# Four reorderings in a hybrid encoder layer: the state recurrence before the within-chunk sums, residual rows loaded tile by tile, a fifth transpose before the first products, and one root for the last four tiles of the first FFN

## The chip, the cores and the metric

The kernel runs on one core of one Trainium2 chip. The metric is the device time of one execution in microseconds (us); less is better. The engines are named as the profile names them: PE is TensorE (matmul), PEld its weight load, DVE is VectorE, ACT is ScalarE, POOL is GpSimd, SP is SyncE, which issues the DMA transfers.

## The reference

One layer works on 1024 rows of 1024 float32 values.

```python
h = h + 0.5 * swiglu(rmsnorm(h, g1), w_gate1, w_up1, w_down1)      # first FFN, width 2816
n = rmsnorm(h, g_mix); z = n @ w_in
# z -> c_q (256) | c_kv (128) | k_rope (32) | u (512) | gate_attn (1024) | gate_ssm (1024)
attn = mla_attention(c_q, c_kv, k_rope)                            # 8 heads, not causal
# S5: 32 groups of 16 inputs, 64 complex states each, in both directions of the sequence
x_t = B u_t;  s_t = lam * s_{t-1} + x_t;  y_t = Re(C s_t);  y = y_fwd + y_bwd + D * u
ssm = glu(gelu(y) @ w_glu + b_glu)
h = h + (sigmoid(gate_attn) * (attn @ w_oa) + sigmoid(gate_ssm) * (ssm @ w_os)) @ w_out
h = h + 0.5 * swiglu(rmsnorm(h, g2), w_gate2, w_up2, w_down2)      # second FFN
out = rmsnorm(h, g_final)
```

## The kernel before

The sequence is cut into 8 tiles of 128 rows (ST = 8), the width into 8 blocks of 128 (KT = 8). A float32 product is made of three passes over operands split into a high part, rounded for the PE, and a low part, the rest (`three_passes`, lines 48 to 50): hi times hi, hi times lo, lo times hi. ACT makes high parts (copies), DVE or POOL low parts (subtractions). All orders are written out by hand, one program per engine, and semaphores link them. DMA transfers all go out on SP's one queue. The phases run one after the other with a barrier between them:

- **First FFN** (`ffn_phase`, 0 to 727 us). A Strassen-like scheme of seven products with operands in blocks. At its start the rows are normalised: squares on ACT (L904), variance on DVE (L371), a root on ACT (L375), one Newton step of five small instructions on DVE (L98 to L102), and the scaling of a tile (`scaled`, L1069). Tiles 0 to 3 are turned (transposed by PE, L1343) as they are, tiles 4 to 7 enter sums of blocks that POOL makes (`combine`, L1310 to L1315). PE's order is: two blocks of tiles 0 to 3 turned, product (0,0), product (0,2), sums of tile 4 turned, product (1,0), sums of tile 5, product (1,2), sums of tiles 6 and 7, then the first whole matrix (`matrix(0)`). The second FFN is the same function with `loaded` set: tiles 0 to 3 come normalised from the phase before it, and tiles 4 to 7 take one root together.
- **Projection** (`project_phase`, 727 to 832 us). `Norm` turns eight tiles in the order 4, 5, 6, 7, 0, 1, 2, 3, counted as turns 0 to 7. Turns 0 to 3 need no scaling first. `RowProduct` multiplies by rows of the weight, a unit (one block of 128) at a time. For its first four units PE does the tiles of the first four turns, with turns 4 to 7 put in between, then the rest of the tiles.
- **SSM** (`ssm_phase`, 832 to 1087 us). Chunks of 8 rows (T = 8), 128 chunks. PE transposes u, makes the chunk states (L1697, ACT writes them into H by L1735 and L1736), and the sums within a chunk, 8 quarters of them (`within`, L1709; DVE adds them to u, L1793). DVE runs the recurrence over chunks: 127 steps of three dependent instructions (L1800, L1802, L1804). ACT (`forward`, L1752) and DVE (`backward`, L1811) then lay the states out for PE's output product y (L1724). Beside this, 16 gate products (`side`, a `ColumnProduct` of 48 matmuls each) go through PE; each needs a sigmoid on ACT (L1628), a high part two products ahead (`high`, ACT L165), a low part on POOL (L173) and stores of the gates. C_mat, which shares its space with M, the matrix of the within sums, is loaded by one transfer of 4 MB (L1678) when the within sums are done; SP issues the gates' stores after it.
- **Mixer** (attention, 1087 to 1458 us), not touched.
- **Merge** (`merge_phase`, 1458 to 1605 us). For each of 8 blocks PE multiplies the attention by w_o_attn (`woa`, 24 matmuls), DVE multiplies by a gate (L2539) and adds the SSM part (L2542); a slot of psum is free for product n + 2 when the gate is multiplied in. Then w_out, 16 units of 24 matmuls. The residual rows (`rows`) come back from DRAM (`kept`) by one transfer of 4 MB (L2468) in SP's second round, and are first read at unit 8 (`add`, L2454).
- **Second FFN** (1605 to 2279 us).

Of the kernel before, what the change touches and what calls it, by code (L numbers as in the profile page):

```python
# [32 lines left out]
P = 128  # L33
# [3 lines left out]
ST = SEQ // P  # L37
# [230 lines left out]
class Norm:  # L268
# [22 lines left out]
    def act(self, act, rp):  # L291
        rest = slice(0, ST - self.AHEAD)
        self.act_square(act, ST - self.AHEAD - 1)
        self.act_high(act, 0)
        act.wait_ge(self.s_var, 1)
        act.activation(self.stat[:, 2, rest], self.stat[:, 1, rest], ACT.Sqrt).then_inc(self.s_sqrt, 1)
        for i in range(1, self.AHEAD):
            self.act_high(act, i)
        for n in range(2):
            rp.high(act, n)  # L300
        for i in range(self.AHEAD, ST):
            self.act_high(act, i)
            if i < ST - 2:
                rp.high(act, i - 2)
# [23 lines left out]
    def dve(self, dve, rp):  # L328
        st, rest = self.stat, slice(0, ST - self.AHEAD)
        dve.wait_ge(self.s_sq, 1)  # L330
        dve.tensor_scalar(st[:, 1, rest], st[:, 0, rest], 1.0 / D, EPS, ALU.mult, ALU.add).then_inc(self.s_var, 1)
        self.dve_low(dve, 0)
        dve.wait_ge(self.s_sqrt, 1)
        newton(Chain(dve, self.s_rstd), st[:, 1, rest], st[:, 2, rest], st[:, 3, rest], st[:, 4, rest])
        dve.wait_ge(self.s_gain, 16)
        self.dve_rows(dve, 4)
        for i in range(1, self.AHEAD):
            self.dve_low(dve, i)
        rp.low(dve, 0)
        self.dve_rows(dve, 5)  # L340
        rp.low(dve, 1)
        for i in range(self.AHEAD, ST):
            self.dve_low(dve, i)
            if i < ST - 2:
                self.dve_rows(dve, i + 2)
                rp.low(dve, i - 2)
# [362 lines left out]
def ffn_phase(nc, tag, gain, w_gate, w_up, w_down, rows, ident, psum, hidden, residual, x=None, finish=None, tables=None, ahead=0, following=None, loaded=None):  # L709
# [10 lines left out]
    with Phase(nc) as ctx:  # L720
# [177 lines left out]
        def _(act):  # L898
# [11 lines left out]

            def lows_high(i):
                for m in range(QUAD):
                    act.wait_ge(s_tr, low_turned(m, i))
                    act.copy(B_hi[:, LOW_BLOCKS[i], :, tile(m)], blocks(LOW_BANKS[i][m])).then_inc(s_bhi, 1)
# [67 lines left out]
            if not ahead:  # L982
                squares(0)
                squares(1)
# [3 lines left out]
            if loaded:  # L988
                square(ST - 1)
                norm.root(act, 0, slice(QUAD, ST))  # L990
            else:
                high(0, 0)
                squares(2)
# [3 lines left out]
            if not loaded:  # L997
                squares(3)
# [57 lines left out]
        def _(dve):  # L1056
# [60 lines left out]
            if loaded:  # L1117
                dve.wait_ge(s_sq, SQUARES)
                norm.var(dve, 0, slice(QUAD, ST))
                norm.inverse(dve, 0, slice(QUAD, ST))  # L1120
                scaled(QUAD)
                scaled(QUAD + 1)
            else:
                low(0, 0)
                normalised(2)
            lows_low(1)
            low(0, 2)
            if loaded:
                scaled(QUAD + 2)
                scaled(QUAD + 3)  # L1130
            else:
                normalised(3)
# [326 lines left out]
def project_phase(nc, w, rows, ident, psum, nT_hi, nT_lo, u, kept, latent_rows, trig_rows, E_dram, carry):  # L1459


    with Phase(nc) as ctx:
# [114 lines left out]
        def _(pe):  # L1577
            ahead, rest = norm.TILES[:norm.AHEAD], norm.TILES[norm.AHEAD:]
            for i in range(norm.AHEAD):
                norm.pe(pe, i)  # L1580
            for n in range(rp.S):
                if n == 0:
                    pe.wait_ge(norm.s_lo, norm.AHEAD)
                rp.tiles(pe, n, ahead, rest[-1])
                for i in ((4,), (5,), (6, 7), ())[n]:
                    norm.pe(pe, i)
# [50 lines left out]
GATES_AFTER = (13, 14, None, 15)  # L1637


def ssm_phase(nc, w, rows, rows_at, ident, psum, nT_hi, nT_lo, u, gates, kern_dram, C_dram, lam8_dram):  # L1640
# [5 lines left out]
    with Phase(nc) as ctx:  # L1646
# [19 lines left out]
        def _(sp):  # L1666
            side.gp.load(sp, 0)
            sp.dma_start(Db, w["ssm_d"][0:1, :].rearrange("a (g i) -> a g i", i=SG).broadcast_to([P, GROUPS, SG])).then_inc(s["d"], 16)
# [4 lines left out]
            sp.dma_start(lam8[:].rearrange("p a b g -> p (a b g)"), lam8_dram).then_inc(s["lam"], 16)  # L1673
# [8 lines left out]
        def _(pe):  # L1682
# [20 lines left out]
            for q in range(NQ):  # L1703
                if q < 4:
                    pe.wait_ge(s["ec"], 2 * (2 * NQ - 3 + q))
                else:
                    pe.wait_ge(s["wadd"], q - 3)
                for g in range(4 * q, 4 * q + 4):
                    mm = pe.matmul(psum[:, 4 + q % 4, g % 4 * P:(g % 4 + 1) * P], UT[:, g, :], M[:, g, :], start=True, stop=True)  # L1709
                mm.then_inc(s["within"], 1)  # L1710
            pe.wait_ge(s["wadd"], NQ)
            for n in range(1, GATES_FIRST):
                side.gp.product(pe, n)
# [16 lines left out]
        def _(act):  # L1730
# [27 lines left out]
            for n in range(GATES_FIRST - 1):  # L1758
                side.sigmoid(act, n)
                if n == GATES_FIRST - 5:  # L1760
# [23 lines left out]
        def _(dve):  # L1784
# [4 lines left out]
            for q in range(NQ):  # L1789
# [6 lines left out]
            for n in range(CH - 1):  # L1796
# [7 lines left out]
                dve.tensor_tensor(H[:, n + 1], H[:, n + 1], prod[:, 1, ::-1], ALU.add).then_inc(s["scan"], 1)  # L1804
            dve.wait_ge(s["scan"], CH)
# [603 lines left out]
def merge_phase(nc, w, psum, rows, kept, woa, held, loaded, gates, partial, gain):  # L2409

    with Phase(nc) as ctx:
# [16 lines left out]
        s_sum, s_hi, s_lo, s_kept = sem("sum"), sem("hi"), sem("lo"), sem("kept")  # L2428
# [26 lines left out]

        def bank(i, half):
# [3 lines left out]
        def _(sp):  # L2460
            for n in range(KT):
# [5 lines left out]
                if n == 1:  # L2467
                    sp.dma_start(rows[:], kept.rearrange("(m p) d -> p m d", p=P)).then_inc(s_kept, 16)  # L2468
# [3 lines left out]
            for u in range(2, NU):  # L2472
                load(sp, u)
                if u == 2:
# [54 lines left out]
        def _(dve):  # L2529
# [19 lines left out]
            for u in range(2, NU):  # L2549
                low(dve, u)  # L2550
                if u == KT:
                    dve.wait_ge(s_kept, 16)
# [10 lines left out]
                if u in (KT + 4, KT + 5):  # L2563
                    i = u - KT - 4
                    dve.wait_ge(s_sq, 2 * i + 2)
                    norm.var(dve, i, slice(2 * i, 2 * i + 2))
            for i in range(QUAD):
# [102 lines left out]
```

## Time and profile before

| | |
|---|---|
| median of 3 runs | 2278.45 us (2277.05 to 2278.88) |
| the profiled execution | 2281.39 us, its span 2279.3 us |
| PE busy | 2150.0 us, 94% of the span, 10074 matmuls |
| DVE busy | 1468.7 us, 64% |
| ACT busy | 918.1 us, 40% |
| POOL busy | 611.4 us, 27% |
| DMA | 263.00 MB, mean 115 GB/s |

The profile gives each instruction's start, duration, engine and line, and for an idle stretch the engine or transfer that ended it. PE is the busiest engine in every phase; what an edit is worth is read from the stretches in which PE stands idle.

### The profile page before, as it was taken

The page shows a single profiled execution, that of the slowest core. Times are in us where ns is not written, and L with a number is a line of the kernel's source. Part 1 is how long each engine was busy: PE and PEld are TensorE (multiplying, and loading weights), DVE is VectorE, ACT ScalarE, POOL GpSimd, SP SyncE. Part 2 cuts the span into 40 slices and gives each one's busy share as a digit, 9 for nine tenths or more (in the row PEclk, how much of TensorE's full clock was granted, in tenths as well). Part 3 has the DMA queues.
Part 4 walks back from the last instruction along what each step waited for, and adds up shares of the span by engine and source line. Part 5 has one row for each costly group of instructions (what it writes and reads, how often), then busy time and mean ns, then how long its engine had stood idle before and what let it go on. Part 6 is the DMA issues. An engine that isn't in the chain of part 4 may idle for free. (4 is left out here: it accounts for less than half of the span.)

```text
span 2279.3 us, 27668 instructions
## 1 busy us (share of the span) xinstructions
PE 2150.0 (94%) x10074; PEld 1778.2 (78%) x10074; DVE 1468.7 (64%) x2300; ACT 918.1 (40%) x1551; POOL 611.4 (27%) x510
## 2 busy tenths in 40 slices
PE   5899999999998999959899999889899999999997
PEld 4778888887887998848777887778678888887886
DVE  7787667657777426951457887554766565657777
ACT  5423333324445342124426778422532323224444
POOL 5336877740000021201002333100533333310000
PEclk9999999999998999979999999999999999999999
DMA  3423334349333455311430000273123232349333
GB/s 120 107 89 122 118 117 139 122 171 339 97 112 114 135 86 163 97 42 55 131 130 25 7 6 15 93 257 126 56 88 120 88 121 88 120 148 342 101 97 111
DMA packets 234471, 263.00 MB, mean 115 GB/s; under 512 B 34720, under 2 KB 169376, under 8 KB 233824
## 3 DMA queue, kind: packets, MB, share of 16 engines
q1 hardware_dynamic: 234336, 261.23, 36.1%
q8 instruction: 81, 1.33, 0.2%
q14 instruction: 54, 0.44, 0.1%
HBM read 184.60 MB, written 76.58 MB: 115 GB/s over the span
## 5 line engine op out<-in xcount | busy, mean ns | idle before, releaser
L48 PE MATMUL psum<-f_B_hi,f_A_hi 128*128 128x512 f32 x1232 | 488.4, 396 | 24.7 <-DVE f_A_lo L1053 12.9
L50 PE MATMUL psum<-f_B_hi,f_A_lo 128*128 128x512 f32 x1232 | 483.3, 392 | 0.0
L49 PE MATMUL psum<-f_B_lo,f_A_hi 128*128 128x512 f32 x1232 | 483.0, 392 | 0.0
L48 PEld LDWEIGHTS psum<-f_B_hi,f_A_hi 128*128 128x128 f32 x1232 | 233.5, 190 | 76.5 <-DVE f_A_lo L1053 20.1
L50 PEld LDWEIGHTS psum<-f_B_hi,f_A_lo 128*128 128x128 f32 x1232 | 233.3, 189 | 49.4
L49 PEld LDWEIGHTS psum<-f_B_lo,f_A_hi 128*128 128x128 f32 x1232 | 233.6, 190 | 47.6
L939 ACT CAST f_A_hi<-f_S 128x512 fp32r<-128x512 f32 x176 | 109.3, 622 | 348.4 <-PE psum L50 340.3
L48 PE MATMUL psum<-f_wd,f_hh 128*128 128x512 f32 x616 | 240.4, 390 | 3.6 <-DVE f_wd L1099 3.6
L50 PE MATMUL psum<-f_wd,f_hh 128*128 128x512 f32 x616 | 240.4, 390 | 0.0
L49 PE MATMUL psum<-f_wd,f_hh 128*128 128x512 f32 x616 | 240.3, 390 | 0.0
L1328 POOL TENSOR_TENSOR f_S<-f_raw 128x512 f32<-128x512 f32 x86 | 129.9, 1511 | 304.4 <-DVE f_A_lo L1053 284.2
L973 ACT CAST f_hh<-f_h_raw 128x512 fp32r<-128x512 f32 x154 | 96.0, 623 | 240.4 <-PE psum L50 230.3
L1053 DVE TENSOR_TENSOR f_A_lo<-f_raw,f_A_hi 128x512 fp32r<-128x512 f32 x132 | 134.8, 1022 | 69.4 <-ACT f_A_hi L939 68.6
L1097 DVE TENSOR_TENSOR f_hh<-f_h_raw,f_hh 128x512 fp32r<-128x512 f32 x154 | 106.6, 692 | 105.0 <-ACT f_hh L973 104.1
L1053 DVE TENSOR_TENSOR f_A_lo<-f_S,f_A_hi 128x512 fp32r<-128x512 f32 x176 | 142.9, 813 | 3.6 <-ACT f_A_hi L939 2.6
L48 PEld LDWEIGHTS psum<-f_wd,f_hh 128*128 128x128 f32 x616 | 116.1, 188 | 28.6 <-DVE f_wd L1099 4.4
L939 ACT CAST f_A_hi<-f_raw 128x512 fp32r<-128x512 f32 x132 | 81.9, 620 | 137.0 <-PE psum L50 135.2
L50 PEld LDWEIGHTS psum<-f_wd,f_hh 128*128 128x128 f32 x616 | 116.0, 188 | 24.2
L49 PEld LDWEIGHTS psum<-f_wd,f_hh 128*128 128x128 f32 x616 | 116.0, 188 | 24.1
L48 PE MATMUL psum<-nT_hi,ga_hi 128*128 128x512 f32 x256 | 103.1, 403 | 24.2 <-POOL ga_lo L173 23.4
L2262 DVE TENSOR_TENSOR mx_PT_lo<-psum,mx_PT_hi 128x512 fp32r<-128x512 f32 x128 | 87.8, 686 | 47.4 <-ACT mx_PT_hi L2126 46.9
L1099 DVE TENSOR_TENSOR f_wd<-f_wd_raw,f_wd 128x512 fp32r<-128x512 f32 x154 | 105.7, 686 | 0.0
(335 smaller groups left out, 4191.7 us busy)
## 6 DMA issues: line engine op xcount, KB each, us to landing
f_h_raw<-hidden SPq DMA_DIRECT2D x154, 256.0 KB, 2.6
hidden<-rows SPq DMA_DIRECT2D x44, 768.0 KB, 4.7
f_raw<-ffn_w_gate SPq DMA_DIRECT2D x44, 512.0 KB, 5.2
f_raw<-ffn_w_up SPq DMA_DIRECT2D x44, 512.0 KB, 5.0
f_wd_raw<-ffn_w_down SPq DMA_DIRECT2D x44, 512.0 KB, 8.9
rows<-x SPq DMA_DIRECT2D x16, 512.0 KB, 7.4
ga_raw<-w_in SPq DMA_DIRECT2D x16, 512.0 KB, 4.6
gates<-ga_sig SPq DMA_DIRECT2D x32, 256.0 KB, 2.3
```

The costliest lines, as they stand in the source:

```text
L48: pe.matmul(out, lhs_hi, rhs_hi, start=first, stop=False, skip_group_check=go_on)
L49: pe.matmul(out, lhs_hi, rhs_lo, start=False, stop=False, skip_group_check=go_on)
L50: return pe.matmul(out, lhs_lo, rhs_hi, start=False, stop=last, skip_group_check=go_on)
L939: act.copy(A_hi[:, q], src).then_inc(s_hi, 1)
L973: act.copy(hh[v % 2][0][:], h_raw[v % 8][:]).then_inc(s_dhi, 1)
L1053: eng.tensor_tensor(A_lo[:, q], src, A_hi[:, q].bitcast(F32), ALU.subtract).then_inc(s_lo, 1)
L1097: dve.tensor_tensor(hh[v % 2][1][:], h_raw[v % 8][:], hh[v % 2][0][:].bitcast(F32), ALU.subtract).then_inc(s_dlo, 1)
L1099: dve.tensor_tensor(wd[v % 2][1][:], wd_of(q, k), wd[v % 2][0][:].bitcast(F32), ALU.subtract).then_inc(s_dlo, 1)
L1328: pool.tensor_tensor(S[:, i], a, b, op).then_inc(s_sum, 1)
L2262: dve.tensor_tensor(pt(PT_lo, g, x), turned_bank(x), pt(PT_hi, g, x).bitcast(F32), ALU.subtract).then_inc(s["tr_lo"], 1)
```

## The change

**First FFN.** An ACT Sqrt of one column stands ahead of the first squares, so that the root's table is loaded there. The variance, root and Newton step of tiles 4 and 5 and those of tiles 6 and 7 become one of each for the four tiles, after all four squares.

**Projection.** Turn 4 is done before the first unit, and one turn follows each of the first three units (before: one, one, two). ACT and DVE follow that order.

**SSM.** The recurrence starts when the states are there; the eight within additions on DVE stand inside it, after steps 10 to 13 and 28 to 31. On PE gate product 1 stands between the fourth and the fifth quarter of the within sums, and products 2 to 12 no longer wait for the additions. lam is loaded second instead of after ten other transfers. On ACT the first two `forward` stand after sigmoid 11 (before: after sigmoid 8).

**Merge.** The residual rows come as eight transfers of 0.5 MB: tiles 0 to 3 in rounds 4 to 7, tiles 4 to 7 with units 7 to 10.

```diff
 class Norm:                                  # projection
-        for n in range(2):
-            rp.high(act, n)
         for i in range(self.AHEAD, ST):
+            rp.high(act, i - self.AHEAD)
             self.act_high(act, i)
-            if i < ST - 2:
-                rp.high(act, i - 2)
...
-        rp.low(dve, 0)
-        self.dve_rows(dve, 5)
-        rp.low(dve, 1)
         for i in range(self.AHEAD, ST):
+            rp.low(dve, i - self.AHEAD)
+            if i + 1 < ST:
+                self.dve_rows(dve, i + 1)
             self.dve_low(dve, i)
-            if i < ST - 2:
-                self.dve_rows(dve, i + 2)
-                rp.low(dve, i - 2)
...
-            for i in range(norm.AHEAD):
+            for i in range(norm.AHEAD + 1):
                 norm.pe(pe, i)
...
-                for i in ((4,), (5,), (6, 7), ())[n]:
-                    norm.pe(pe, i)
+                if norm.AHEAD + 1 + n < ST:
+                    norm.pe(pe, norm.AHEAD + 1 + n)
 ffn_phase, ACT (first FFN: loaded is None)
+            def other_squares():
+                for m in range(ST - 1 if loaded else QUAD, ST):
+                    square(m)
+                norm.root(act, 0 if loaded else 2, slice(QUAD, ST))
...
             if not ahead:
+                act.activation(stat[:, 2, 0:1], ident[:, 0:1], ACT.Sqrt)
                 squares(0)
                 squares(1)
             lows_high(0)
-                squares(2)
+            other_squares()
             lows_high(1)
...
-            if not loaded:
-                squares(3)
 ffn_phase, DVE
-                normalised(2)
+            dve.wait_ge(s_sq, SQUARES)
+            norm.var(dve, 0 if loaded else 2, slice(QUAD, ST))
+            norm.inverse(dve, 0 if loaded else 2, slice(QUAD, ST))
+            scaled(QUAD)
+            scaled(QUAD + 1)
             lows_low(1)
             low(0, 2)
-                normalised(3)
+            scaled(QUAD + 2)
+            scaled(QUAD + 3)
 ssm_phase
+WITHIN_AFTER = (10, 11, 12, 13, 28, 29, 30, 31)
...
             for q in range(NQ):
+                if q == NQ // 2:
+                    side.gp.product(pe, 1)
...
-            pe.wait_ge(s["wadd"], NQ)
-            for n in range(1, GATES_FIRST):
-                side.gp.product(pe, n)
+            for n in range(2, GATES_FIRST):
+                side.gp.product(pe, n)
+            pe.wait_ge(s["wadd"], NQ)
...
                 side.sigmoid(act, n)
-                if n == GATES_FIRST - 5:
+                if n == GATES_FIRST - 2:
                     forward(0)
                     forward(1)
...
+                if n in WITHIN_AFTER:
+                    within(WITHIN_AFTER.index(n))
 merge_phase, SP
+        def take(sp, m):
+            sp.dma_start(rows[:, m, :], kept[m * P:(m + 1) * P, :]).then_inc(s_kept[m // QUAD], 16)
...
-                if n == 1:
-                    sp.dma_start(rows[:], kept.rearrange("(m p) d -> p m d", p=P)).then_inc(s_kept, 16)
+                if n >= QUAD:
+                    take(sp, n - QUAD)
...
+                if KT - 1 <= u < KT + 3:
+                    take(sp, u - KT + 1 + QUAD)
```

ACT in the SSM phase, before: sigmoids of the gates (`ga_sig`), high parts of the gate weights (`ga_hi`) and the four copies of `forward` (`rows<-ss_H`). The first sigmoid row shown is that of product 8.

```order
L1628 ACTIVATE ga_sig<-psum 128x512 x2
L165 CAST ga_hi<-ga_raw 128x1024
L1752 COPY rows<-ss_H 64x128x8 x4
L1628 ACTIVATE ga_sig<-psum 128x512 x2
L165 CAST ga_hi<-ga_raw 128x1024
```

The same engine after the change, from the sigmoid of product 10 on.

```order
L1618 ACTIVATE ga_sig<-psum 128x512 x2
L165 CAST ga_hi<-ga_raw 128x1024
L1618 ACTIVATE ga_sig<-psum 128x512 x2
L165 CAST ga_hi<-ga_raw 128x1024
L1745 COPY rows<-ss_H 64x128x8 x4
L1618 ACTIVATE ga_sig<-psum 128x512 x2
L165 CAST ga_hi<-ga_raw 128x1024
```

The four copies have moved down past three pairs of sigmoid and high part, so that the high parts for products 11, 12 and 13 no longer stand behind them.

SP in the merge phase, before, from its second round on: gates, the SSM part (`mg_part`), w_o_attn (`woa_raw`), the residual rows and w_out (`mg_wo_raw`).

```order
L2464 DMA mg_gate<-gates 128x1024
L2465 DMA mg_part<-partial 128x1024
L157 DMA woa_raw_11138<-w_o_attn 128x4x128
L2468 DMA rows<-kept 128x8x1024
L2464 DMA mg_gate<-gates 128x1024
L2465 DMA mg_part<-partial 128x1024
L157 DMA woa_raw_11139<-w_o_attn 128x4x128
```

SP in the same phase after the change, from the fifth round on; in the second there is no such row any more.

```order
L2462 DMA mg_gate<-gates 128x1024
L2463 DMA mg_part<-partial 128x1024
L157 DMA woa_raw_11124<-w_o_attn 128x4x128
L2452 DMA rows<-kept 128x1024
L2462 DMA mg_gate<-gates 128x1024
L2463 DMA mg_part<-partial 128x1024
L2452 DMA rows<-kept 128x1024
```

The rows' 4 MB no longer stand between the gates of block 1 and those of block 2; one tile goes out in each of the last four rounds.

DVE at the start of the first FFN after the change, from the low part of product (0,0) on (before, a second set of variance and Newton rows, L371 and L98 to L102, stood ahead of the last row here, and these rows were 128x2).

```order
L1048 TENSOR_TENSOR f_A_lo<-f_raw_74,f_A_hi 128x512
L365 TENSOR_SCALAR f_stat<-f_stat 128x4
L98 RECIPROCAL f_stat<-f_stat 128x4
L99 TENSOR_TENSOR f_stat<-f_stat 128x4
L100 TENSOR_TENSOR f_stat<-f_stat 128x4
L101 TENSOR_SCALAR f_stat<-f_stat 128x4
L102 TENSOR_TENSOR f_stat<-f_stat 128x4
L1064 SCALAR_TENSOR_TENSOR rows<-rows,f_stat,f_gb 128x1024 x2
L1077 TENSOR_TENSOR f_B_lo<-psum,f_B_hi 128x4x128 x4
L1048 TENSOR_TENSOR f_A_lo<-f_raw_74,f_A_hi 128x512
L1064 SCALAR_TENSOR_TENSOR rows<-rows,f_stat,f_gb 128x1024 x2
```

The second Newton step is gone, and its tiles are scaled straight after the low part of product (0,2).

## Rows read from the trace of the kernel before

**Rows 1.** Longest wait of PE in the SSM phase: total, times, longest (us).

```profile
PE psum L48 <- POOL ga_lo L173: 23.4, 1, 23.4
```

**Rows 2.** Timeline of the SSM phase: start, duration (us), engine, operation, [idle before, releaser].

```profile
865.77 7.30 PE L1709 MATMUL psum<-ss_C_mat,ss_UT 128*128 128x128 f32 x64
...
873.93 0.50 PE L48 MATMUL psum<-nT_hi,ga_hi 128*128 128x512 f32 x1 [0.85 <-DVE u L1793]
...
1010.05 0.79 PE L48 MATMUL psum<-nT_hi,ga_hi 128*128 128x512 f32 x1 [23.40 <-POOL ga_lo L173]
...
1035.12 3.73 PE L1724 MATMUL psum<-ss_C_mat,rows 128*128 128x128 f32 x32
...
857.75 0.58 ACT L1736 COPY ss_H<-psum 64x512 f32<-64x512 f32 x1
...
888.99 1.17 ACT L1628 ACTIVATE ga_sig<-psum 128x512 f32<-128x512 f32 x2 [21.00 <-DMA gates<-ga_sig]
...
998.40 7.34 ACT L1752 COPY rows<-ss_H 64x1024 f32<-64x1024 f32 x4 [32.17 <-DVE ss_H L1804]
...
873.11 0.37 SPq L1678 DMA_DIRECT2D ss_C_mat<-C_dram  x1
873.52 16.98 SPq L1612 DMA_DIRECT2D gates<-ga_sig  x4
...
891.17 2.40 POOL L173 TENSOR_TENSOR ga_lo<-ga_raw,ga_hi 128x1024 fp32r<-128x1024 f32 x1 [20.73 <-ACT ga_hi L165]
...
873.19 0.69 DVE L1793 TENSOR_TENSOR u<-psum,u 128x512 f32<-128x512 f32 x1 [0.20 <-PE psum L1709]
873.80 0.28 DVE L1800 TENSOR_TENSOR ss_prod<-ss_H,ss_lam 128x128 f32<-128x128 f32 x1
```

**Rows 3.** Busy times in the recurrence's stretch: PE, PEld, DVE, ACT, POOL, clock, DMA, GB/s.

```profile
873.80:998.40 124.60, 112.72 (x480) 90.32 (x480) 111.54 (x383) 16.27 (x25) 19.37 (x8) 0.97 0.34 106
```

**Rows 4.** The recurrence's first instruction: ns min/median/max, first and last start (us).

```profile
L1800 DVE TENSOR_TENSOR ss_prod<-ss_H,ss_lam x127: 281/293/2479, 873.8 to 997.5; 128x128 f32<-128x128 f32 x127
```

**Rows 5.** Timeline of the merge phase, then the w_out matmuls (ns min/median/max, starts).

```profile
1469.33 1.08 SPq L2468 DMA_DIRECT2D rows<-kept  x1
...
1489.47 1.22 DVE L2539 TENSOR_TENSOR mg_val<-psum,mg_gate 128x1024 f32<-128x1024 f32 x1 [9.37 <-DMA mg_gate<-gates]
...
1490.84 0.77 PE L48 MATMUL psum<-aT_hi,woa_hi 128*128 128x512 f32 x1 [7.73 <-DVE mg_val L2539]
...
L48 PE MATMUL psum<-mg_wo_hi,mg_mT_hi x128: 389/389/389, 1515.5 to 1601.9; 128*128 128x512 f32 x128
```

**Rows 6.** Busy times in ten us of the merge, columns as in rows 3.

```profile
1475.00:1485.00 10.00, 8.11 (x36) 6.38 (x34) 4.88 (x5) 2.58 (x4) 0.00 (x0) 1.00 1.03 406
```

**Rows 7.** Timeline of the projection, PE.

```profile
742.73 1.03 PE L360 MATMUL psum<-ident,pjn_xn 128*128 128x128 f32 x8
743.52 0.45 PE L48 MATMUL psum<-rp_hi,nT_hi 128*128 128x448 f32 x1
...
747.86 0.47 PE L48 MATMUL psum<-rp_hi,nT_hi 128*128 128x448 f32 x1 [0.79 <-DVE rp_lo L242]
...
754.97 0.47 PE L48 MATMUL psum<-rp_hi,nT_hi 128*128 128x448 f32 x1
```

**Rows 8.** Timeline of the first FFN's start, ACT, DVE and PE.

```profile
21.19 1.06 ACT L904 ACTIVATE f_dump<-rows 128x1024 f32<-128x1024 f32 x1
22.15 0.19 ACT L904 ACTIVATION_READ_ACCUMULATOR f_dump<-rows 128x1 f32 x1
...
23.80 2.48 DVE L1069 SCALAR_TENSOR_TENSOR rows<-rows,f_stat,f_gb 128x1024 f32<-128x1024 f32 x2
...
57.95 0.47 PE L48 MATMUL psum<-f_B_hi,f_A_hi 128*128 128x512 f32 x1 [1.76 <-DVE f_B_lo L1087]
```

**Rows 9.** Timeline of the second FFN's start, DVE and PE.

```profile
1612.11 2.48 DVE L1069 SCALAR_TENSOR_TENSOR rows<-rows,f_stat,f_gb 128x1024 f32<-128x1024 f32 x2
...
1640.32 0.47 PE L48 MATMUL psum<-f_B_hi,f_A_hi 128*128 128x512 f32 x1 [1.19 <-DVE f_B_lo L1087]
```

More of the change, by code:

```diff
@@ L987, in _ @@
             lows_high(0)
[L988 to L991, printed above, removed]
+            if not loaded:
                 high(0, 0)
-                squares(2)
+            other_squares()
             lows_high(1)
@@ L1116, in _ @@
             lows_low(0)
[L1117 to L1123, printed above, removed]
-                low(0, 0)
-                normalised(2)
+            if not loaded:
+                low(0, 0)
+            dve.wait_ge(s_sq, SQUARES)
[3 more added lines that the diff above has]
+            scaled(QUAD + 1)
             lows_low(1)
             low(0, 2)
[L1128 to L1131, printed above, removed]
-                normalised(3)
+            scaled(QUAD + 2)
+            scaled(QUAD + 3)
             low(1, 0)
@@ L1667, in _ @@
             side.gp.load(sp, 0)
+            sp.dma_start(lam8[:].rearrange("p a b g -> p (a b g)"), lam8_dram).then_inc(s["lam"], 16)
             sp.dma_start(Db, w["ssm_d"][0:1, :].rearrange("a (g i) -> a g i", i=SG).broadcast_to([P, GROUPS, SG])).then_inc(s["d"], 16)
@@ L1672, in _ @@
             side.gp.load(sp, 1)
-            sp.dma_start(lam8[:].rearrange("p a b g -> p (a b g)"), lam8_dram).then_inc(s["lam"], 16)
             side.gp.load(sp, 2)
@@ L1788, in _, with within @@
             dve.memset(H[:, 0], 0.0).then_inc(s["scan"], 1)
-            for q in range(NQ):
+            def within(q):
                 g = slice(4 * q, 4 * q + 4)
@@ L2427, in merge_phase @@
         s_g, s_p = [sem("g0"), sem("g1")], [sem("p0"), sem("p1")]
-        s_sum, s_hi, s_lo, s_kept = sem("sum"), sem("hi"), sem("lo"), sem("kept")
+        s_sum, s_hi, s_lo, s_kept = sem("sum"), sem("hi"), sem("lo"), [sem("kept0"), sem("kept1")]
         NU = 2 * KT
@@ L2551, in _ @@
                 if u == KT:
-                    dve.wait_ge(s_kept, 16)
+                    dve.wait_ge(s_kept[0], 16 * QUAD)
                     for i in range(QUAD):
@@ L2566, in _ @@
                     norm.var(dve, i, slice(2 * i, 2 * i + 2))
+            dve.wait_ge(s_kept[1], 16 * QUAD)
             for i in range(QUAD):
```

## Prediction

> **What bounds the kernel now.** I read the busy times first: PE is busy for 94% of the span, so time can only come from where PE stands idle. The lists of waits, phase by phase, name two large holes: 23.4 us in the SSM phase, ended by a low part of the gate weights [rows 1], and 7.73 us in the merge, ended by a gate multiplication on DVE [rows 5]. I then followed both back on the timelines, and after them the small holes at the starts of the projection and of the first FFN. The reader should see that neither of the large holes is made by the engine named as its releaser.
>
> In the SSM phase, gate product 11 starts at 1010.05. Its weights need ACT's high part, which ACT makes after sigmoid 9; but ACT had waited 32.17 us in front of `forward` for the end of the recurrence at 998.4, and then copied for 7.34 us [rows 2]. So PE's hole is the recurrence's end, and the recurrence began only at 873.80, after the within additions, although the states were there at 858.33 (857.75 + 0.58) [rows 2].
>
> In the merge, the multiplication waited until 1489.47 for its gates; these had been issued behind the 4 MB of residual rows of 1469.33 [rows 5].
>
> **The change part by part: the SSM phase.** PE's work stays the same; I lay it out again from the first within sum at 865.77 [rows 2]. One gate product is 112.72/10 = 11.27 us [rows 3], all within sums are 7.30 [rows 2].
>
> 1. Removed: the hole of 23.40, and the 0.85 before product 1, where PE waited for the last addition [rows 2]. PE can put product 1 between the quarters, as its low part was ready in time before too, and the fifth quarter needs psum banks that DVE frees after recurrence steps 10 to 13.
> 2. The recurrence is on nobody's path any more. It now starts at 858.4. Its step is 0.85 us where POOL is idle (three instructions of which the first is 0.29 [rows 4], with the gaps between them); 127 steps are 107.3. It took 124.6 [rows 3]: the 17.3 above that belong to the 8 POOL instructions in that stretch [rows 3], 2.16 each, and one first instruction took 2479 ns instead of 293 [rows 4]. Starting earlier it meets 11 of them: 858.4 + 107.3 + 11 x 2.16 + 8 additions of 0.69 [rows 2] = 995. The additions at steps 10 to 13 come at about 870 to 875, the others at about 890, both after PE has made their sums and before PE needs the banks again.
> 3. Added, a wait that the edit doesn't mention. The load of C_mat must wait for the last within sum, which now stands behind product 1: 11.27 later, at 884.4 instead of 873.11 [rows 2]. The gates' stores are queued behind that load on SP. Before, sigmoid 1 waited for the store of gates 0 until 888.99, after 21.00 us of idling, though the store was issued at 873.5 [rows 2]; its low part for product 3 was done at 891.17 + 2.40 = 893.57 [rows 2]. All of that moves by 11.27, to 904.84. Product 2 ends at 865.77 + 7.30 + 2 x 11.27 = 895.6. So PE stands idle for 9.2 us ahead of product 3. Before, product 2 ended at 873.93 + 22.54 = 896.47, 2.9 us after the low part was done.
> 4. The clock. After the hole of 23.40, products 11 and 12 took 1035.12 - 1010.05 = 25.07 [rows 2] where two full-speed ones take 22.54: 2.5 us at the lower of TensorE's two levels. The new hole should cost the same, so this cancels. If 9.2 us of idling cost nothing, there are 2.5 more to gain.
> 5. `forward` now follows sigmoid 11. Product 11 ends at 1008.7, the sigmoid and high part take 2.1, so the first pair of copies is done at about 1014.5 and all four at 1018.2. PE wants the first pair when product 12 ends.
>
> The y products then start at 865.77 + 7.30 + 12 x 11.27 + 9.2 + 2.5 = 1020.0 instead of 1035.12: **15.1 us**. If the store did not have to wait for the load, it would be 24.3, or 26.8 with the clock; that is the upper bound. What follows y is tied to it by the same waits as before and moves along.
>
> The Trainium skill (DMA: Bandwidth & Descriptors, "Queues, rings and completion order") says that descriptors of one issuing engine's row are consumed in ring order on each DMA engine, while a later transfer's completion need not come after an earlier one's. By the first half the wait of 9.2 us stands in full; by the second the gates' small store could get out earlier and the 24.3 would hold. The trace agrees with the first half here: the store took until 888.99. I give the second case little.
>
> **The merge.** Without the 4 MB, gates 2 stand behind the 2.5 MB of the first two rounds, issued from 1466.5 on. At 406 GB/s [rows 6] these and the 1.25 MB of the third round take 9.2 us from about 1467, so gates 2 land by 1478. DVE was through with block 1 at 1489.47 - 9.37 = 1480.1 [rows 5]; it can multiply by 1481.3, before product 3 ends at 1483.1 (1490.84 - 7.73) [rows 5]. The hole of 7.73 goes. After it, products 4 to 7 took 1515.5 - 1490.84 = 24.7 [rows 5]; 96 matmuls at the pace of w_out's, (1601.9 - 1515.5)/127/3 = 0.227, are 21.8. The 2.9 are the lower clock and go too. Together **10.6 us**. The eight small loads go out in rounds whose data are 1.5 MB or less per 5.4 us and are needed 50 us later; they are hidden. If gates 2 or 3 still came late, half of it would remain: I bound this part by 5 and 11.
>
> **The projection.** The fifth turn moves into the gap while PE waits for the first low part, at no cost: its scaled rows exist by then. From 742.73 to 754.97 PE now does four turns of 0.79 (743.52 - 742.73), three units of some 2.55, and holes of 0.79 and about 0.6 [rows 7]. After the change it does three turns, and since scaling and low parts run one turn ahead, each is ready when PE asks, by my walk through the waits: the tightest is the low part of the fourth unit, at 750.0 for 750.3. That is 0.8 + 0.8 + 0.5 = **2.1 us**, a little rounded down. Bounds: 0.8 (only the turn) and 3.5 (with less time at the lower clock before it).
>
> **The first FFN.** The table load that moves is hidden by the waiting for x, except some 0.3 us at the end of the first root's chain. The single root makes tile 4 later and tiles 6 and 7 sooner. ACT adds two squares, 1.25 us each (22.15 + 0.19 - 21.19) [rows 8], so the scaling of tile 4 starts at 23.80 + 2.5 - 0.3 = 26.0. How long from there to the first whole matrix? The second FFN already runs in this order: 1640.32 - 1612.11 = 28.2 [rows 9]. That gives 54.2 instead of 57.95 [rows 8]: **3.7 us**. Bounds: 1, if POOL's chain of block sums, which starts 2.2 later, binds more here, and 5. If the late tile 4 is all that counts, it is a loss of 2.2.
>
> **Sum.** 15.1 + 10.6 + 2.1 + 3.7 = 31.5 us. The profiled execution (2281.39, span 2279.3) would come to 2249.9; it stands 2.9 above the median. From the median, 2278.45 - 31.5 = **2247**.
>
> **The rivals.**
> - *The store gets past the load* (no wait for product 3). For it: nothing in the trace. 2278.45 - 31.5 - 9.2 = 2238, with the clock 2235. 0.07.
> - *The first FFN pays for its late tile 4*: 2247 + 3.7 + 2.2 = 2253. For it: PE is idle right before product (0,2), which needs no tile 6 or 7. Against it: [rows 9]. 0.12.
> - *The merge keeps a wait*, because w_out's and the part's transfers delay the gates: 2247 + 5 = 2252, at most 2256. 0.09.
> - *The other side: the recurrence still binds, and later than before.* It would have to end so late that y starts 31.5 after 1020.0, at 1051.5; with 3.7 for the first two copies that is an end at 1047.8, a recurrence of 189 us instead of 136.6. Its 381 instructions would have to be 0.14 us longer each, through POOL or through additions waiting inside it. From 1016.3 on (1020.0 - 3.7) each us is lost; above 1047.8 the kernel is slower than before, e.g. 2283 at 1052. Against it: the steps' times [rows 3, 4]. 0.02.
>
> **How the numbers follow.** My forecast, all parts within some us of the sum, has 0.68, with a range of its own of 2241 to 2252; the rest (0.02) is what I have not thought of. What a measurement can tell from no change is about 0.2%, 4.6 us. To leave out no more than 2 in 10, the range goes from 2238 (the store free) to 2256 (a merge wait or a loss in the FFN). Faster 0.96, within 0.2% 0.02, slower 0.02.
>
> **What would show it.** In the changed kernel: no wait above 1 us for product 11, a wait of about 9 us for product 3, ended by POOL's low part, and ahead of it ACT waiting for a gates transfer until about 900; the recurrence from 858 to 995; y at 15 us less distance from the first within sum; no wait in the merge's products; the projection's rest starting 10.1 after its first unit ends; the first whole matrix near 54. The prediction fails if the wait for product 3 is absent or much longer, or if the recurrence ends after 1016.

## The result, and the profile of the changed kernel

The changed kernel takes 2244.39 us (median of 4 runs, 2243.45 to 2245.89), the kernel before 2277.84 us beside it (4 runs, 2277.05 to 2278.88). The ratio is 0.9854, with a 95% interval of 0.9836 to 0.9871: 33.45 us less, 31.5 forecast. The profiled execution (2243.45 us, span 2241.4) is 37.9 us shorter in span than before's profiled one. The 4.45 us between 33.45 and 37.9 are taken up below.

TensorE's waits in the SSM phase come first, engine and line, then the releaser: us in total, times, longest. They answer to [rows 1]. The SSM phase begins at 825.36 us here and at 832.93 in before, so 7.6 us have to be added to a time of this phase to set it beside the forecast's.

```profile
PE psum L48 <- POOL ga_lo L173: 9.1, 1, 9.1
PE psum L1678 <- PEq L69: 1.5, 1, 1.5
```

The hole of 23.4 us is gone and one of 9.1 stands in its place, ended by the same line. The timeline of the same phase shows that it is another one (it answers to [rows 2]).

```profile
861.33 0.61 PE L1702 MATMUL psum<-ss_C_mat,ss_UT 128*128 128x128 f32 x4
861.70 0.48 PE L48 MATMUL psum<-nT_hi,ga_hi 128*128 128x512 f32 x1
...
897.07 0.80 PE L48 MATMUL psum<-nT_hi,ga_hi 128*128 128x512 f32 x1 [9.09 <-POOL ga_lo L173]
...
1011.01 0.50 PE L1717 MATMUL psum<-ss_C_mat,rows 128*128 128x128 f32 x3
...
876.77 0.37 SPq L1669 DMA_DIRECT2D ss_C_mat<-C_dram  x1
877.18 16.83 SPq L1602 DMA_DIRECT2D gates<-ga_sig  x4
...
892.49 1.17 ACT L1618 ACTIVATE ga_sig<-psum 128x512 f32<-128x512 f32 x2 [32.06 <-DMA gates<-ga_sig]
893.56 1.04 ACT L165 CAST ga_hi<-ga_raw 128x1024 fp32r<-128x1024 f32 x1
...
894.67 2.34 POOL L173 TENSOR_TENSOR ga_lo<-ga_raw,ga_hi 128x1024 fp32r<-128x1024 f32 x1 [31.80 <-ACT ga_hi L165]
...
1001.87 7.82 ACT L1745 COPY rows<-ss_H 64x1024 f32<-64x1024 f32 x4
```

Read it backwards from 897.07: product 3 waits for POOL's low part of 894.67, this for ACT's high part, ACT for the landing of the gates' first store, and that store was issued at 877.18, just behind the 4 MB load of C_mat at 876.77. The sigmoid that waits for it starts 15.3 us after its issue. The load was issued when the last within sum was done, and this now stands behind product 1 (861.70). The first copies (L1745) no longer wait for anything: the recurrence had ended by then.

The recurrence's first instruction (ns min/median/max, first and last start; as [rows 4]), and VectorE's copies that follow its end:

```profile
L1793 DVE TENSOR_TENSOR ss_prod<-ss_H,ss_lam x127: 280/293/2499, 850.9 to 984.9; 128x128 f32<-128x128 f32 x127
...
985.71 4.74 DVE L1806 COPY rows<-ss_H 64x1024 f32<-64x1024 f32 x4
```

It lasts 985.7 - 850.9 = 134.8 us. The forecast was 136.6.

Then busy times and granted clock (columns as in [rows 3]) of the first product behind the hole and of the last 25 us of products:

```profile
897.10:908.40 11.30, 11.30 (x43) 9.04 (x44) 10.18 (x33) 1.04 (x1) 2.40 (x1) 0.86 0.37 108
985.70:1011.00 25.30, 25.30 (x109) 20.34 (x108) 4.74 (x4) 11.72 (x10) 4.80 (x2) 1.00 0.29 84
```

The projection's start (as [rows 7]) and the first whole matrix of the first FFN (as the last of [rows 8]), TensorE's timeline:

```profile
54.08 0.47 PE L48 MATMUL psum<-f_B_hi,f_A_hi 128*128 128x512 f32 x1 [1.19 <-DVE f_B_lo L1082]
...
724.40 6.17 PE L354 MATMUL psum<-ident,rows 128*128 128x128 f32 x32 [4.71 <-PEq L69]
732.12 1.07 PE L354 MATMUL psum<-ident,pjn_xn 128*128 128x128 f32 x8 [1.55 <-DVE nT_lo L323]
734.91 0.44 PE L48 MATMUL psum<-rp_hi,nT_hi 128*128 128x448 f32 x1 [1.73 <-DVE rp_lo L242]
```

The fifth turn (732.12) stands ahead of the first unit (734.91), and the unit's wait is 1.73 us. In the merge TensorE's list of waits has one row left, the phase change; the 7.73 of [rows 5] is absent:

```profile
PE psum L48 <- PEq L69: 1.2, 1, 1.2
```

### The profile page after: what moved, and what is told of

Read it like the earlier page. It is cut to its first block and busy times, and to the rows that moved or that the text cites. A ratio compares the mean times of both kernels' runs of the same rounds, so it can differ in the third digit from the quotient of the medians.

```text
span 2241.4 us, 27668 instructions
## 1 busy us (share of the span) xinstructions
PE 2140.1 (95%) x10074; PEld 1770.1 (79%) x10074; DVE 1468.3 (66%) x2294; ACT 917.6 (41%) x1550; POOL 611.3 (27%) x510
```

## The experiments

Twelve kernels, each timed beside the kernel before. Each profile also gives the lengths of the stages, from one phase's first TensorE instruction to the next one's, so a stage that an experiment leaves alone is measured again by it. The expectations stand as they were written ahead of the runs.

**1. The SSM part alone** (p1): before, with the change's hunks of the SSM phase.

```diff
+                if q == NQ // 2:
+                    side.gp.product(pe, 1)
...
-                if n == GATES_FIRST - 5:
+                if n == GATES_FIRST - 2:
                     forward(0)
...
+                if n in WITHIN_AFTER:
+                    within(WITHIN_AFTER.index(n))
```

> Before, with the change's SSM part alone. Theory A (the parts are separate holes of TensorE and add up): the y products start 16.6 us sooner after the first within sum, as in the changed kernel, with a wait of about 9 us for gate product 3; the kernel gains 15.1 (forecast) to 16.6 us. Theory B (the parts lean on each other, as by the clock or by transfers): less than 13 or more than 19 us, and the rest of the 33.5 us is spread otherwise over the other three kernels of this set.

Measured: 2260.49 us against 2277.02, ratio 0.9928 (0.9914 to 0.9941), 16.5 us. Its profile has a wait of 8.49 us for product 3. Theory A. Behind that wait product 3 takes 13.97 us (903.35 to 917.32, granted clock 0.79), where in the changed kernel it takes 12.73 behind 9.09 us of idling (897.07 to 909.79, clock 0.88) and at full clock 11.25.

**2. The merge part alone** (p2).

```diff
-                if n == 1:
-                    sp.dma_start(rows[:], kept.rearrange("(m p) d -> p m d", p=P)).then_inc(s_kept, 16)
+                if n >= QUAD:
+                    take(sp, n - QUAD)
...
+                if KT - 1 <= u < KT + 3:
+                    take(sp, u - KT + 1 + QUAD)
```

> Before, with the residual rows tile by tile alone. Theory A: the wait of 7.73 us in the merge's products is gone and the clock stays up behind it; w_out's products start 10.6 to 10.8 us sooner after the merge's first product; gain 10.6 us. Theory B (only the wait goes, the granted clock is low there anyway): 7.7 us.

Measured: 2268.76, ratio 0.9964 (0.9951 to 0.9976), 8.3 us, which by itself lies between the two theories. The merge's products run from 1466.61 to w_out's first at 1504.77 without a wait, 38.2 us, as in the changed kernel. The other executions show what 10.6 was made of. The first product behind the hole, in p1, where the merge is as in before:

```profile
1471.75 0.76 PE L48 MATMUL psum<-aT_hi,woa_hi 128*128 128x512 f32 x1 [6.97 <-DVE mg_val L2544]
```

There the wait is 6.97 us and the four products behind it take 23.7 (to 1495.49), while in before's profile they are 7.73 and 24.7 [rows 5]. Over the eight profiles with the old merge, its first product to the second FFN's first turn is 139.17 us in before's and 137.25 to 137.61 in the seven others; over the five with the new one 128.3 to 128.4. The gain is 9.1 us from a usual execution and 10.8 only from the one that was profiled. The extra 1.7 us of before's profile lie in the clock behind the hole: 0.88 over its 24.7 us (p1: 0.91 over 23.75), and the four products there take 23.3 to 23.9 us in the seven others. So theory A is right in its mechanism (the wait and the clock both go), and its size is 9.1.

**3. The projection part alone** (p3).

```diff
-            for i in range(norm.AHEAD):
+            for i in range(norm.AHEAD + 1):
                 norm.pe(pe, i)
...
+            rp.low(dve, i - self.AHEAD)
+            if i + 1 < ST:
+                self.dve_rows(dve, i + 1)
             self.dve_low(dve, i)
```

> Before, with the projection's fifth turn sooner alone. Theory A (what the changed kernel's profile showed belongs to this edit: a shorter wait for the first low part and a first unit at the full granted clock): 4.2 us. Theory B (the full clock there was that one execution's, or comes from elsewhere): the forecast's 2.1 to 2.3 us. The profile's first unit tells it: 2.7 us long by A, 4.6 by B.

Measured: 2271.94, ratio 0.9981 (0.9972 to 0.9990), 5.1 us; the stage is 100.93 us long, where the eight profiles without the new order of turns have 104.7 to 105.5 (mean 105.2). The first unit takes 2.5 us (738.29 to the turn at 740.79), as theory A has it; 4.2 us by the stage.

**4. The first FFN's part alone** (p4).

```diff
+                act.activation(stat[:, 2, 0:1], ident[:, 0:1], ACT.Sqrt)
...
-                squares(2)
+            other_squares()
...
-                squares(3)
...
-                normalised(2)
...
+            norm.inverse(dve, 0 if loaded else 2, slice(QUAD, ST))
...
-                normalised(3)
```

> Before, with the first FFN's single root and early table load alone. Theory A (forecast): the first whole matrix starts at about 54.1 instead of 57.95, gain 3.4 to 3.9 us. Theory B (what the FFN gains at its start is partly given back by its end, as the changed kernel's projection started only 3.4 us sooner): 3 us or less.

Measured: 2275.33, ratio 0.9993 (0.9984 to 1.0002), 1.7 us and not told apart from nothing. The whole matrix starts at 54.31, as theory A has it, but the projection's first turn is at 725.59, 2.2 us sooner than in before. Over all profiles that turn is at 726.75 to 729.08 (mean 727.75, eight without the single root) and at 724.40 to 725.80 (mean 724.98, six with the single root): 2.8 us. A's start of the matrix is there, and the gain is B's (3 us or less); why some of it is not seen at the end of the phase, which B calls given back, is not shown.

**5. The copies' place alone** (s1): one line of before. It asks whether the recurrence had to start sooner at all.

```diff
-                if n == GATES_FIRST - 5:
+                if n == GATES_FIRST - 2:
                     forward(0)
                     forward(1)
```

> Before, with one edit alone: the copies of the states for the y products move on ScalarE from behind sigmoid 7 to behind sigmoid 10, two sigmoids later than they now ask for the end of the recurrence; the recurrence stays behind the within sums, as in before. Theory A (the 23.4 us hole was only ScalarE's queue; the recurrence at 998.4 is soon enough for everyone else): gate product 11 starts at about 986.7, product 12 ends at 1009.2, the y products follow without a wait, so 1035.1 - 1009.2 = 25.9 us gained and no new wait for product 3, since the load of C_mat keeps its place: 2251. Theory B (the recurrence has to start early, as the change makes it): the end at 998.4 is now waited for by the y products or their copies, and the gain is that of the SSM part alone, 16.5 us, or less: 2260 or more.

(In the kernel's own count, from 0, the copies move from behind sigmoid 8 to behind sigmoid 11.)

Measured: 2252.55 against 2278.15, ratio 0.9891 (0.9874 to 0.9908), 25.6 us. This one line gives more than the change's whole SSM part. In its timeline:

```profile
1008.67 0.42 PE L1724 MATMUL psum<-ss_C_mat,rows 128*128 128x128 f32 x2
...
1004.50 2.03 ACT L1752 COPY rows<-ss_H 64x1024 f32<-64x1024 f32 x1 [4.86 <-DVE ss_H L1804]
```

and of the recurrence's stretch (columns as in [rows 3]):

```profile
873.50:1004.46 130.96, 130.84 (x559) 105.20 (x560) 117.93 (x382) 22.31 (x33) 26.69 (x11) 1.00 0.40 125
```

TensorE works through, and the y products start at 1008.67. The copies still wait 4.86 us for the recurrence, but nobody waits for the copies. It is close: the recurrence ends at 1004.5 instead of 998.4, since with the hole gone it meets 11 POOL instructions instead of 8 [rows 3], (130.96 - 124.60)/3 = 2.1 us each; two copies of 1.96 (7.82 for four in the changed kernel) then end at 1008.4, 0.3 before y. Theory A, with almost no margin. The opposite single edit, the early recurrence with the copies left where they were, was not run, so what it would give alone is not shown.

**6. Sums first** (s2): the changed kernel, the within sums' additions at the recurrence's first steps.

```diff
-WITHIN_AFTER = (10, 11, 12, 13, 28, 29, 30, 31)
+WITHIN_AFTER = (0, 1, 2, 3, 8, 9, 10, 11)
...
-                if q == NQ // 2:
-                    side.gp.product(pe, 1)
...
-            for n in range(2, GATES_FIRST):
+            for n in range(1, GATES_FIRST):
```

> The changed kernel, with the additions of the within sums at steps 0 to 3 and 8 to 11 of the recurrence instead of 10 to 13 and 28 to 31, and gate product 1 behind all within sums again. The last within sum, and with it the load of C_mat, comes about 11 us sooner. Theory A (product 3 waits because the gates' store is queued behind the load of C_mat): the wait of 9.1 us for product 3 goes, and 1.3 us of lower clock with it: 2244.4 - 10.4 = 2234. Theory B (the store or its sigmoid is slow for another reason, e.g. the eleven POOL instructions that meet the recurrence): the wait stays where it is, 2243 to 2245, or only part of it goes.

Measured: 2234.71 against 2278.15, ratio 0.9811 (0.9796 to 0.9826), 9.7 us below the changed kernel's median (which was taken in another set, with before at 2277.84). SP's and ACT's rows:

```profile
869.48 0.37 SPq L1669 DMA_DIRECT2D ss_C_mat<-C_dram  x1
869.89 1.70 SPq L1602 DMA_DIRECT2D gates<-ga_sig  x2
...
885.71 1.17 ACT L1618 ACTIVATE ga_sig<-psum 128x512 f32<-128x512 f32 x2 [23.23 <-DMA gates<-ga_sig]
```

The sigmoid still starts 15.8 us after the store's issue, but both are early enough: the low part is done at 890.35 (887.89 + 2.46), product 2 ends at 891.77, and no product waits. The within sums pay 1.1 us in three small waits. Theory A.

**7. C_mat in four pieces behind the stores** (s3): the changed kernel, only SP's queue differs.

```diff
...
-            sp.dma_start(C_mat[:], C_dram.rearrange("c p g x -> p c g x")).then_inc(s["c"], 16)
-            side.sync(sp)
+            for b in range(BLOCKS):
+                if b >= 2:
+                    side.gp.load(sp, b + 2)
+                side.store(sp, b)
+                at = slice(PB * b, PB * b + PB)
+                sp.dma_start(C_mat[:, :, at], C_dram.rearrange("c p g x -> p c g x")[:, :, at]).then_inc(s["c"], 16)
+            side.sync(sp, BLOCKS)
...
-            pe.wait_ge(s["c"], 16)
+            pe.wait_ge(s["c"], 16 * BLOCKS)
```

> The changed kernel, with the 4 MB load of C_mat issued in four pieces of 1 MB, one behind each of the gates' stores 0 to 3, instead of whole ahead of them. Theory A (as in the run before, the store waits in the queue for the load): no wait above 1 us for product 3, the y products 10.4 us sooner: 2234. Theory B (4 MB beside the gates' stores delay them wherever they stand): the wait is only moved, to products 4 to 6, in pieces of 2 to 3 us: 2238 to 2244.

Measured: 2233.57, ratio 0.9806 (0.9791 to 0.9820), 10.8 us below the changed kernel's median and the fastest kernel of this study. Its queue, ACT and TensorE:

```profile
877.01 0.81 SPq L1602 DMA_DIRECT2D gates<-ga_sig  x2
877.87 0.46 SPq L1674 DMA_DIRECT2D ss_C_mat<-C_dram  x1
...
879.12 0.60 ACT L1618 ACTIVATE ga_sig<-psum 128x512 f32<-128x512 f32 x1 [18.45 <-DMA gates<-ga_sig]
...
1000.52 0.39 PE L1722 MATMUL psum<-ss_C_mat,rows 128*128 128x128 f32 x2
```

The same store, issued at nearly the same time (877.01 for 877.18), now lets the sigmoid start after 2.1 us instead of 15.3, and TensorE runs from the first within sum to y without a stop. Theory A; B's small waits are absent.

**8. The rest of the change with before's SSM phase and the one line of s1** (s4).

> The changed kernel's projection, first FFN and merge, with the SSM phase of before but for the copies for the y products, which stand behind sigmoid 10. Theory A (as above: the early recurrence buys nothing): 25.9 - 16.6 = 9.3 us below the changed kernel, 2235. Theory B (the early recurrence is needed): 2244 or above.

Measured: 2237.07, ratio 0.9822 (0.9807 to 0.9836), 7.3 us below the changed kernel; y starts at 1001.45, the copies wait 4.86 us for the recurrence. Theory A, 2 us above its figure. These 2 us do not lie in the SSM phase, which is as long as in s1 (228.68 us both times); in this profile the second FFN and its end take 674.2 us, the most of all fourteen.

**9 and 10. The first FFN's two edits apart** (t1: the early table load, t2: the single root).

```diff
+                act.activation(stat[:, 2, 0:1], ident[:, 0:1], ACT.Sqrt)
```

> Before, with the first FFN's table load ahead of its squares alone (one small square root on ScalarE before x is there). Theory A (forecast: hidden but for some 0.3 us): first whole matrix at about 57.6 instead of 57.95. Theory B (the table load was on the path to the first rows, as TensorE's first turn came 1.1 us sooner in the changed kernel): first turn at 10.7 instead of 11.8, whole matrix at about 56.9, gain 1.1 us.

> Before, with the single root for tiles 4 to 7 of the first FFN and without the early table load. Theory A (the two edits add up to 3.85 us at the first whole matrix, and the table gives 0.3): 54.4. Theory B (the table gives 1.1): 55.2, so 2.8 us. Theory C (the late tile 4 costs what the single root saves): 57 or later.

Measured: t1 2278.13 against 2277.54, ratio 1.0007 (0.9998 to 1.0016); t2 2276.44, ratio 0.9991 (0.9982 to 1.0001). Neither is told apart from no change, so I go by the profiles. TensorE's first turn and first whole matrix in t1, and the whole matrix in t2:

```profile
10.80 1.67 PE L1344 MATMUL psum<-ident,rows 128*128 128x128 f32 x5 [10.80 <-DVE rows L1070]
...
57.98 0.47 PE L48 MATMUL psum<-f_B_hi,f_A_hi 128*128 128x512 f32 x1 [1.76 <-DVE f_B_lo L1088]
```

```profile
54.38 0.47 PE L48 MATMUL psum<-f_B_hi,f_A_hi 128*128 128x512 f32 x1 [1.21 <-DVE f_B_lo L1087]
```

The early table load brings the first turn one us forward, and the whole matrix stays where it was (57.98 for 57.95): what starts sooner waits longer for the rest. The single root alone gives 57.95 - 54.38 = 3.6 us. Of t1, B's first turn came and its 1.1 us did not; A's 0.3 can't be told, as the whole matrix starts anywhere from 57.36 to 58.13 in the eight profiles without the single root. Of t2, A holds and C falls.

**11. TensorE's order of turns alone** (t3): only the loop of the projection's TensorE program, ScalarE's and VectorE's orders stay.

> Before, with the projection's order of turns on TensorE alone (the fifth ahead of the first unit, one more ahead of each of the next); ScalarE's and VectorE's orders stay. Theory A (TensorE's wait of 4.7 us ahead of the first unit is what brings the lower clock, and the turn breaks it up): the first unit is 2.7 us long instead of 4.6, and with the turn hidden 2.7 of the part's 4.2 us are there. Theory B (the clock needs the other engines' order too, since the first low part comes at the same time by it): the first unit stays at 4.6 us, and the gain is 0.8 us. Theory C (the low parts come one turn too late for this order): new waits at units 2 and 3, gain under 2.7.

Measured: 2273.31, ratio 0.9984 (0.9974 to 0.9993), 4.2 us, and a stage of 100.92 us: all of the projection's gain. The first unit in before and in t3 (columns as in [rows 3]):

```profile
738.30:742.70 4.40, 4.40 (x12) 3.95 (x13) 1.59 (x2) 0.00 (x0) 0.00 (x0) 0.52 1.02 254
```

```profile
739.60:742.10 2.50, 2.50 (x13) 2.28 (x14) 2.50 (x3) 0.00 (x0) 0.00 (x0) 1.00 1.02 287
```

Before, TensorE stands idle for 4.7 us, and then its twelve matmuls run at a granted clock of 0.52, the lower of its two levels. With a turn in the middle of that idle time, waits of 1.39 and 1.73 us are left and the clock is 1.00. It is no accident of one execution: from its first matmul to the next turn the first unit takes 4.1 to 4.6 us in all eight profiles with before's order of turns and 2.50 to 2.55 in all six with the new one. Theory A's mechanism, but 4.2 where I gave it 2.7: the holes at the later units go too, with no help from the other engines' orders.

**12. The residual rows late, in one piece** (t4).

```diff
-                if n == 1:
+                if n == 6:
                     sp.dma_start(rows[:], kept.rearrange("(m p) d -> p m d", p=P)).then_inc(s_kept, 16)
```

> Before, with the whole 4 MB load of the residual rows issued in the merge's seventh round instead of its second, in one piece. Theory A (only its place ahead of the gates matters, not its size): no wait for gate product 3 of the merge, its stage 9.1 us shorter than in before's typical executions (137.4 us from the merge's first product to the second FFN's first turn), as with the rows tile by tile: 2269. Theory B (4 MB in one piece holds up what is queued behind it, w_out's weights): the wait comes back there, 2272 or above.

Measured: 2270.46, ratio 0.9970 (0.9960 to 0.9979), 7.1 us. No wait in the merge's products, but one in w_out's, whose stage is 130.29 us long, 1.9 more than with the rows tile by tile:

```profile
1509.29 0.50 PE L48 MATMUL psum<-mg_wo_hi,mg_mT_hi 128*128 128x512 f32 x1 [1.66 <-DVE mg_val L2539]
```

Theory A holds for the products, and theory B's wait is there too, at a fifth of the size. The place ahead of the gates was 7 of the 9 us (137.5 to 130.3); the rest belongs to the 4 MB in one piece: issued at 1490.61, it has the last gates behind it (1495.21), and VectorE waits 3.85 us for these until 1508.01.

## Why the prediction was right, step by step

The stages, from the profiles (us):

| stage | without the part | with it | gain | forecast |
| --- | --- | --- | --- | --- |
| first FFN, start to the projection's first turn | 727.75 (8) | 724.98 (6) | 2.8 | 3.7 |
| projection, to the SSM phase's first turn | 105.20 (8) | 101.10 (5) | 4.1 | 2.1 |
| SSM phase, to the mixer's first turn | 254.61 (8) | 238.58 (2) | 16.0 | 15.1 |
| merge's first product to the second FFN's first turn | 137.67 (8) | 128.35 (5) | 9.3 | 10.6 |
| sum | | | 32.2 | 31.5 |

In brackets the number of profiles behind each mean; for the merge before's own 139.17 is among them. The timed 33.45 us has an interval of about 29 to 37, which holds both sums. The four parts' own timed gains are 16.5, 8.3, 5.1 and 1.7, together 31.6 us, so nothing shows that the parts lean on each other.

- **SSM, steps 1 and 3: right.** No wait for product 11, one of 9.09 us for product 3 (9.2 forecast). Its cause is shown: with the load of C_mat sooner (s2: 42.0 us after the phase's first turn instead of 51.4) or behind the stores (s3) the wait is gone, and the time falls by 9.7 and 10.8 us. The rival "the store gets past the load" fell. The Trainium skill (DMA: Bandwidth & Descriptors, "Queues, rings and completion order") has the descriptors of one issuing engine's row consumed in ring order on each DMA engine; the pair of s3 and the changed kernel agrees: from the store's issue to the sigmoid that waits for it are 2.1 us ahead of the load and 15.3 behind it.
- **Step 2: right, and more than needed.** The recurrence took 134.8 us, 136.6 forecast, and nobody waits for it. What I did not see is that its earlier start buys little: in s1 the whole hole goes (25.6 us with its clock) by the place of the copies in ScalarE's queue alone. In the changed kernel the new order is even the reason for the loss, as it puts product 1 ahead of the last within sums and so the load of C_mat behind it. What it can give, with the queue mended, is read from s3 against s4: y starts 174.88 us after the phase's first turn in s3 and 176.02 in s4, 1.1 us, of which 0.85 are the wait of [rows 2]; and margin, since in s1 the first two copies are done 0.3 us before y. The two kernels' times differ by more, 3.5 us (2233.57 and 2237.07); in the profiles the larger part of that lies in the second FFN, whose code is the same, and its cause is not shown.
- **Step 4, right within its scatter.** "The new hole should cost the same" in clock, 2.5 us. In the changed kernel's profile product 3 takes 12.73 us where the later ones take 11.25, so the 9.1 us hole cost 1.5, and that is most of the 1.4 us by which the SSM part in the profiles of before and after (16.5) beats the forecast. But in p1 the hole of 8.49 us cost 13.97 - 11.25 = 2.7, and there the stage is 15.7 us shorter than the mean without the part. The old hole of 23.40 cost 1.6 to 2.8 in the eight profiles that have it (product 11 takes 12.84 to 14.01). One execution can't size this term.
- **Step 5: right.** The first copies start at 1001.87, right behind sigmoid 11, at no cost.
- **The merge: right in mechanism, 10.6 for 9.1.** Hole and clock were both read from one execution. In the other seven with that merge the stage is 1.6 to 1.9 us shorter, by a clock that stays low for less time behind the hole; this is part of why before's profiled execution stood above its median. I had taken that excess off the level, but not out of the terms.
- **The projection: the term that failed, 2.1 for 4.1.** I counted the turn and the holes behind the first unit, and left the first unit as it was. The upper bound of 3.5 named the clock and put it too low: t3 shows the clock at 1.00 instead of 0.52. From its first matmul to the next turn the first unit takes 742.73 - 738.30 = 4.43 us before and 2.51 in t3: 1.9 us, and with the 2.1 of the forecast 4.0.
- **The first FFN: 3.7 for 2.8.** The whole matrix started at 54.08, forecast 54.2; the single root alone does it (t2), and the table load adds nothing to be seen at the matrix (t1). In the forecast's sum the bracket for one square, 22.15 + 0.19 - 21.19, is 1.15 and not 1.25; 1.25 is the distance from one square's start to the next, and the scaling of tile 4 did start at 25.86, forecast 26.0. The late tile 4 costs nothing, so that rival fell. About 1 us is not seen at the phase's end. The phase's own scatter (726.75 to 729.08 in eight executions) is larger than that, so whether it is given back stays open.
- **33.45 against 37.9.** The second FFN and its end, the same code in all kernels, take 673.6 us in before's profile, 670.9 in the changed kernel's and 670.9 to 674.2 in all fourteen. So 2.7 of the 4.45 are scatter of that stage, and 1.7 the merge's excess just named.

Errors of opposite sign, the projection's and the SSM part's (too low by 2.0 and 0.9) and the merge's and the FFN's (too high by 1.3 and 0.9), cancelled in part. That the sum came within 2.6 us of the time is luck to that extent; that each of the four holes went as described is not.

## What to carry to other kernels

Before work is moved to end sooner, look at who asks for it: an in-order engine that waits early for a late result makes a hole that one line, the wait's place in the queue, can close. Whenever a step is moved, follow every transfer that its end releases, and what is queued behind it; here a 4 MB load ahead of a small store cost 9 us, and putting it behind in pieces made the best kernel. Size a term from more than one execution where unchanged stages can be had in several profiles.

## What the runs showed of the hardware

- The price of the lower clock behind a hole did not grow in step with the hole, and it scatters from one execution to the next: 1.5 us after 9.1 us of idling (SSM, changed) but 2.7 after 8.5 (p1), 1.6 to 2.8 after the same 23.4 in eight profiles, 1.9 after 6.97 (merge, p1: 23.7 us for four products that take 38.2 x 4/7 = 21.8 in p2) and 2.9 after 7.73 (merge, before), and 1.6 to 2.1 after 4.3 to 4.8 (projection, eight profiles). A turn in the middle of the projection's idle time kept the clock up (1.00 in t3, first unit 2.50 to 2.55 us in all six profiles with it).
- In code that no part touches the granted clock falls in some executions and not in others. Right behind the second FFN's change of weights before's profile shows a low stretch, at about the same point the changed kernel's shows none (columns as in [rows 3], TensorE alone: busy, clock, DMA share, GB/s):

```profile
2050.00:2060.00 10.00, 8.21 (x37) 1.00 1.03 403
2060.00:2070.00 10.00, 10.00 (x39) 0.83 1.04 401
```

```profile
2014.90:2024.90 10.00, 8.21 (x36) 1.00 1.03 403
2024.90:2034.90 10.00, 10.00 (x46) 1.00 1.04 404
```

  The idle 1.79 us ahead of both is the same. That stretch costs 0.17 x 10 = 1.7 us. Each FFN has this hole of 1.79 to 1.80 us once; over the fourteen profiles the granted clock in the ten us behind it is 0.83 in nine of the first FFN and in three of the second, and 1.00 in all others. So executions of the same code differ by some us.
- A step of the recurrence on VectorE that meets a POOL instruction is 2.1 us longer: 8 of them in 124.60 us, 11 in 130.96. POOL's low part is itself 2.34 us long, so VectorE's instruction of 0.29 us, which takes up to 2.50 there, stands still for nearly all of it.
